# Rest of the index stage taken apart among the first projections, second heads moved among the next pair's tiles, TensorE's two long loops written out

## What is computed

```python
q, k, v, ga, qi, ki, wi, u, gb = _project(x, pos, w_in)      # one combined projection, 2048 -> 7248
I[t, s] = sum_h w[t, h] * relu(qi[t, h] . ki[s])              # 16 index heads of width 64
idx = top_k(causal(I), k)                                     # k = 128 (prompt), 256 (samples)
a = softmax(q . k[idx] / sqrt(128)) @ v[idx]                  # 8 heads of 128
p = pool_mix(u)                                               # trailing means, per-group map
y = LayerNorm(alpha * x + w_out @ [a * silu(ga); p * silu(gb)])
```

## Time and profile before

| | us |
|---|---|
| Runs (median, lowest, highest) | 1290.25, 1288.89, 1293.27 |
| Profiled execution | 1291.14 |
| Its span, first to last instruction | 1289.3 |
| Mean granted TensorE clock | 0.966 of full |

### The profile page before, as it was taken

One profiled execution on the slowest core, in us unless ns is written; L12 is line 12 of the kernel. 1 busy time (PEld: TensorE's weight loads), 2 busy tenths in 40 slices (PEclk: granted clock), 3 DMA queues, 4 the chain that ended last, 5 costly groups with the idle time before them and its releaser, 6 DMA issues.

```text
span 1289.3 us, 27399 instructions
## 1 busy us (share of the span) xinstructions
PE 1208.1 (94%) x10300; PEld 1109.7 (86%) x10300; DVE 592.3 (46%) x1080; ACT 358.9 (28%) x664; POOL 348.6 (27%) x150
## 2 busy tenths in 40 slices
PE   7899976989899999989998999999999999999995
PEld 6787755989899989989997888897888979999992
DVE  3555569986118404730763352342432643232326
ACT  4233332213222312232233232322232242212210
POOL 2322210333233323323331122112212223333320
PEclk8999987989999999989998999999999999999996
DMA  8522230322233223313334777667777757322203
GB/s 247 130 73 77 58 89 1 100 75 77 63 100 92 75 73 94 96 54 84 92 89 156 236 259 233 226 229 243 244 245 238 244 180 243 93 83 81 80 0 139
DMA packets 197976, 170.56 MB, mean 132 GB/s; under 512 B 19890, under 2 KB 178538, under 8 KB 196658
## 3 DMA queue, kind: packets, MB, share of 16 engines
q1 hardware_dynamic: 184458, 160.48, 40.2%
q10 hardware_dynamic: 13424, 8.67, 2.4%
HBM read 159.47 MB, written 9.74 MB: 131 GB/s over the span
## 4 chain that ended last, share of the span: by engine, by line
PE 75%; DVE 12%; issue 8%; ACT 2%; DMA 1%; DVEq 0%; ACTq 0%; SPq 0%
PE acc L1008 54%; PE bank L1222 5%; PE bank L1239 3%; PE acc L1312 2%; PE bank L1065 2%; DVE scoreP L1569 2%; DVE top L1565 2%; PE bank L1168 2%; PE bank L1149 1%; PE acc L1366 1%; DVE rot L1496 1%; DVE top L1604 1%; PE acc L1268 1%; DVE scoreS L1607 1%; DVE y L1915 1%
## 5 line engine op out<-in xcount | busy, mean ns | idle before, releaser
L597 POOL TENSOR_TENSOR wL<-rawW,wH 128x1024 fp32r<-128x1024 f32 (+1 forms) x146 | 348.4, 2387 | 892.4 <-ACT wH L619 892.4
L1008 PE MATMUL acc<-actH,wH 128*128 128x272 f32 (+1 forms) x2304 | 497.1, 297 | 10.2 <-issue 9.2
L1008 PE MATMUL acc<-actH,wL 128*128 128x272 f32 (+1 forms) x2304 | 481.4, 291 | 0.0
L1008 PE MATMUL acc<-actL,wH 128*128 128x272 f32 (+1 forms) x2304 | 480.2, 290 | 0.0
L1008 PEld LDWEIGHTS acc<-actH,wH 128*128 128x128 f32 (+1 forms) x2304 | 366.3, 191 | 31.5 <-issue 29.4
L1008 PEld LDWEIGHTS acc<-actL,wH 128*128 128x128 f32 (+1 forms) x2304 | 366.5, 191 | 0.0
L1008 PEld LDWEIGHTS acc<-actH,wL 128*128 128x128 f32 (+1 forms) x2304 | 364.1, 191 | 0.0
L619 ACT ACTIVATE wH<-rawW 128x1024 fp32r<-128x1024 f32 (+1 forms) x146 | 153.8, 1055 | 270.3 <-PE acc L1008 257.2
L1222 PE MATMUL bank<-sq,kPage 128*128 128x128 f32 x512 | 70.8, 282 | 9.0 <-issue 4.9
L1222 PEld LDWEIGHTS bank<-sq,kPage 128*128 128x128 f32 x512 | 56.8, 143 | 21.4 <-issue 16.3
L1627 DVE SCALAR_TENSOR_TENSOR gate<-tanhC,raw 128x544 f32<-128x544 f32 x8 | 5.8, 723 | 146.7 <-ACT raw L810 146.7
(11 more groups left out here) (206 smaller groups left out, 1029.1 us busy)
## 6 DMA issues: line engine op xcount, KB each, us to landing
rawW<-in_w_in SPq DMA_DIRECT2D x112, 512.0 KB, 3.8
kPage<-in_cache_k SPq DMA_DIRECT2D x64, 512.0 KB, 4.7
vPage<-in_cache_v SPq DMA_DIRECT2D x64, 512.0 KB, 4.8
rawW<-in_w_out SPq DMA_DIRECT2D x32, 512.0 KB, 4.0
y<-in_x_prompt SPq DMA_DIRECT2D x4, 1024.0 KB, 9.3
out_y_prompt<-y SPq DMA_DIRECT2D x8, 512.0 KB, 2.8
xnat<-in_x_prompt SPq DMA_DIRECT2D x2, 1024.0 KB, 7.6
xnat<-in_x_prompt ACTq DMA_DIRECT2D x2, 1024.0 KB, 11.2
```

What stands on the lines that cost most here:

```text
L597: pool.tensor_tensor(wL[:, slot, :, 0:width], rawW[:, slot, :, 0:width], wH[:, slot, :, 0:width].bitcast(F32), ALU.subtract).then_inc(stag ...
L1008: last = pe.matmul(acc[t.slot][0:width, e, 0:HT], w[:, u.slot, k, 0:width], a[:, kk, e * HT:(e + 1) * HT], start=(half == 0 and k == 0 and ...
```

## The change

The memory plan is reordered (two holes of 64 and 160 columns are put in) so that the buffers of the pair stage that are used early lie clear of the index stage's. The rest:

```diff
@@ banks: the index rest and the first pair's value transposes share one rotation; every pair has its own
+        zb = banks.stage([..., "R0", "T2", "R1", "T3", "v0", "vs0", "R2", "T4", "R3", "T5",
+                          "R4", "T6", "R5", "T7", "v1", "vs1", "R6", "R7", "Rn", "S0", "S1", "Sn"], four)
@@ SP: gate tiles follow the value tiles
+            for j in range(2):
+                load_tile(w_view, GA0 + j * P, TILE_C + 2 + j)
+            order = ((K0, 0), (Q0, 0), (K0, 1), (Q0, 1), (V0, 2), (V0, 3), (GA0, 2), (GA0, 3))
...
+            sp.wait_ge(exp_ready, 32)
+            key_pages(0, 1, None)
             sp.wait_ge(c_done, 1)
-            key_pages(0, 1, None)
+            key_pages(0, 2, "K3a")
             sp.dma_start(wtab[:], windows).then_inc(wtab_in, 16)
+            mask(0, None)
+            key_pages(0, 3, "K7a")
             unit(4)
@@ ACT: among the index rest
+                if n == 1:
+                    high(TILE_C + 3, 0)
+                    values(0, 0)
+                if n == 3:
+                    copy_tile(1, raw[:, 1])
+                    high(TILE_C + 3, 1)
+                if n == 5:
+                    high(TILE_C + 4, 0)
+                    values(1, 0)
+                if n == 7:
+                    gate_tile(2, 0)
+                    high(TILE_C + 4, 1)
@@ ACT: before the cached attention
-            for m in range(3):
+            copy_tile(0)
+            for m in range(8):
                 key_copied("a", m)
-            key_copied("a", 3)
+            exps(0)
             high(TILE_B + 2, 0)
...
@@ PE: the index rest
+            unit(TILE_C, 0)
...
+            index_products(zb, names[0:2], 1)
+            unit(TILE_C, 1, quarters=(0,))
+            index_products(zb, names[2:4], 1)
+            unit(TILE_C, 1, quarters=(1,))
+            index_products(zb, names[4:6], 1)
+            unit(TILE_C + 1, 0, quarters=(0,))
+            rows_scored(0)
+            unit(TILE_C + 1, 0, quarters=(1,))
+            rows_scored(1)
+            copied(TILE_C)
+            by_token("v", 0, 0, raw[:, 0])
...                       (rows_scored(2) to (7), one quarter between two; v1 after the fifth)
+            unit(TILE_C + 3, 0, quarters=(0,))
             b = zb("Rn") ...
+            unit(TILE_C + 3, 0, quarters=(1,))
             (S0, S1)
+            unit(TILE_C + 3, 1, quarters=(0,))
             (Sn)
+            unit(TILE_C + 3, 1, quarters=(1,))
@@ PE: a pair, written out four times; j = TILE_C + 4 + 8 * i; tiles K0 Q0 K1 Q1 V0' V1' gate0' gate1'
+                unit(j, 0); unit(j, 1); unit(j + 1, 0)
+                pe.wait_ge(head_ready, 4 * i + 2); by_token("k", 0, i, kT[:, 0])
+                unit(j + 1, 1); unit(j + 2, 0)
+                pe.wait_ge(head_ready, 4 * i + 3); scores(0)
+                unit(j + 2, 1); unit(j + 3, 0)
+                pe.wait_ge(head_ready, 4 * i + 4); by_token("k", 1, i, kT[:, 1]); turned(0, 0); turned(0, 1)
+                unit(j + 3, 1); values_of(0, 0); turned(0, 2); values_of(0, 1); turned(0, 3)
+                unit(j + 4, 0); values_of(0, 2); values_of(0, 3)
+                pe.wait_ge(head_ready, 4 * i + 5); scores(1)
+                if last: unit(TILE_B, 1); (all of turned(1, .), values_of(1, .)); return
+                unit(j + 4, 1); unit(j + 5, 0)
+                copied(j + 4); by_token("v", 0, i + 1, raw[:, 0]); turned(1, 0); turned(1, 1)
+                unit(j + 5, 1); values_of(1, 0); turned(1, 2); values_of(1, 1); turned(1, 3)
+                unit(j + 6, 0); values_of(1, 2); values_of(1, 3)
+                copied(j + 5); by_token("v", 1, i + 1, raw[:, 1])
+                unit(j + 6, 1); unit(j + 7, 0); unit(j + 7, 1)
@@ PE: "a" of the cached attention, and the loop over groups
-                if m in (0, 2, 4, 5):
-                    quarter((0, 0, 1, 1, 2, 3)[m])
...
-            with pe.Fori(0, LOOPS) as g:
-                group(g, False)
-            group(LOOPS, True)
+            for g in range(GROUPS):
+                group(g, g == LOOPS)
@@ DVE
-            EARLY = (0, 2, 4)
+            EARLY = (0, 2, 3, 5, 6)
...
+            copied(TILE_C + 2); make_gate(0)          (between R7 and Rn)
...
-            with dve.Fori(0, TOPK_P // ROUND - len(EARLY)) as i:
+            picks(2); copied(TILE_C + 3); make_gate(1); picks(3)
+            rotated(0, kT, 0, 0); picks(3)
+            rotated(1, qT, 0, 0); picks(TOPK_P // ROUND - len(EARLY) - 8)
...                                                   (keepP as before, then the pairs, written out)
+                late = i == 3
+                if i:
+                    rotated(0, kT, 0, i); pick_keys(3)
+                    rotated(1, qT, 0, i); pick_keys(2 if late else 3)
                 softmax(0)
+                rotated(2, kT, 1, i); gated(0, (0, 1)); rotated(3, qT, 1, i); gated(0, (2, 3))
                 softmax(1)
+                if not late:
+                    pick_keys(4)
                 gated(1, range(TT))
+                if not late:
+                    copied(TILE_C + 10 + 8 * i); make_gate(0)
+                    copied(TILE_C + 11 + 8 * i); make_gate(1); pick_keys(1)
```

More of the change, by code:

```diff
@@ new lines, in heads @@
+                keys_out(1)
+                copy_tile(j + 3, qT[:, 1])
+                probs_turned(0, (2, 3))
+                high(TILE_C + j + 5, 1)
+                if last:
+                    act.wait_ge(head_ready, 4 * i + 5)
+                    sample_part(qS, 1, qT)
+                    exps(1)
+                    probs_turned(1, range(TT))
+                    return
+                high(TILE_C + j + 6, 0)
+                act.wait_ge(head_ready, 4 * i + 5)
+                sample_part(qS, 1, qT)
@@ L820, in _ @@
+                high(TILE_C + j + 9, 0)
+                act.wait_ge(gate_ready, 2 * i + 3)
+                gate_tile(j + 7, 1)
+                high(TILE_C + j + 9, 1)
+            for i in range(4):
+                heads(i, i == 3)
             for t in range(TT):
@@ L1089, in pages_turned, with rows_scored, by_token @@
                 full(b, last)
+            def rows_scored(n):
+                b, b2 = zb(f"T{n}"), zb(f"R{n}")
+                dst = take(b2)
+                pe.wait_ge(bank_free[b.slot], b.read)
+                for a in range(PAGES // 2):
+                    last = pe.matmul(dst[:, a * P:(a + 1) * P], kiPT[:, n % 2, a, :],
+                                     qiS[:, :, :, n * NT:(n + 1) * NT].rearrange("p e h t -> p (e h) t"),
+                                     start=True, stop=True)
+                full(b2, last)
+                if n + 2 < NB:
+                    pages_turned(n + 2)
+            def by_token(name, X, i, src):
+                for part, lo, hi in (("", 0, NP_), ("s", NP_, T)):
+                    b = cb(f"{name}{part}{X}", i)
+                    dst = take(b)
+                    for n, at in enumerate(range(lo, hi, P)):
+                        last = pe.transpose(dst[0:min(P, hi - at), n * P:(n + 1) * P], src[:, at:min(at + P, hi)], ident)
+                    full(b, last)
+            unit(TILE_C, 0)
             pe.wait_ge(kip_in, 16 * NB * PAGES)
@@ new lines, in heads @@
+                turned(0, 0)
+                turned(0, 1)
+                unit(j + 3, 1)
+                values_of(0, 0)
+                turned(0, 2)
+                values_of(0, 1)
+                turned(0, 3)
+                unit(j + 4, 0)
+                values_of(0, 2)
+                values_of(0, 3)
+                pe.wait_ge(head_ready, 4 * i + 5)
+                scores(1)
+                if last:
+                    unit(TILE_B, 1)
+                    turned(1, 0)
+                    turned(1, 1)
+                    values_of(1, 0)
+                    turned(1, 2)
+                    values_of(1, 1)
+                    turned(1, 3)
+                    values_of(1, 2)
+                    values_of(1, 3)
+                    return
@@ L1199, in _ @@
+                unit(j + 4, 1)
+                unit(j + 5, 0)
+                copied(j + 4)
+                by_token("v", 0, i + 1, raw[:, 0])
                 turned(1, 0)
                 turned(1, 1)
+                unit(j + 5, 1)
                 values_of(1, 0)
@@ L1616, in _ @@
             own.step(dve.tensor_copy(keepP[:, 0:P], causal))
-            dve.wait_ge(consts_in, 32)
             own.step(dve.tensor_scalar(halfscale[:], halfscale[:], 0.5, None, ALU.mult))
-            rounds = TOPK_S // ROUND // 4
-            with dve.Fori(0, 4) as i:
-                own.enter(i, 2 * rounds + 4 * 3 + 8)
-                def make_gate(X):
-                    dve.scalar_tensor_tensor(gate[:, X, :], tanhC[:], 1.0, raw[:, X, :], ALU.add, ALU.mult
-                                             ).then_inc(gate_ready, 1)
+            own.wait()
+            for i in range(4):
                 def softmax(X):
```

346 lines of the change are left out of this document (180 added, 166 removed).

## The result

The changed kernel takes 1261.8 us (median of 4 runs, 1260.4 to 1263.2) beside 1289.6 us for the kernel before on the same chip: a ratio of 0.977 (0.975 to 0.979). The forecast was 1258.5 us. The profiled executions are 1291.1 and 1260.4 us, with spans of 1289.3 and 1258.6 us; the granted clock rose from 0.966 to 0.976.

A forecast was written before the change was run, and what follows sets the result against it. PE's own line of work was taken to bound the kernel; -18.4 - 19.6 + 6.8 + 5 - 6.5 = -32.7 us took the profiled 1291.14 to 1258.4 us, the median forecast being 1258.5 us, range 1248 to 1270 us.

The forecast's parts named there:

- A: Index rest to the first K1: reordered work removes PE's waits for DVE's sums, -18.4 us (bounds -31 and -12).
- B: Pair loop written out: three stops, the clock after them and waits for probabilities go, -19.6 us (-13 to -21).
- C: One round more before softmax 0 in pairs 1 and 2 makes PE wait for K1, +6.8 us (0 to +8).
- D: "a" without its quarters: thin steps and waits for key pages, +5 us (+1 to +11).
- E: Groups' loop on PE written out: two stops and 1.5 us of clock go, -6.5 us (-5 to -8).
- 59.8 us: DVE's chain from the last sample score, near 240 us, to K1 rotated in the first pair, so at 299.8 us.
- three rotations at 4.8: DVE's rotations before the first K1, POOL beside them at worst, plus gaps: 14.4 us of DVE's chain.
- some 2 us: PE's forecast stand before K0 and again before Q0 in the first pair, with 8 us before K1.
- PE waits 2.6 us in each of two pairs: Wait before K1 in pairs 1 and 2, from one 2.84 us round more before softmax 0.
- 0.8 us each for the clock: Added in pairs 1 and 2 for the lower clock, on top of the 2.6 us wait in each.
- Rival 2: DVE's chain is longer, weighings meeting POOL in the index rest, more low clock, "a" at its upper end: 1267 us, 22%.
- 17 us: Length of "a" from the end of its 4.09 us stop: eight steps 15.2 us, plus waits for pages.

The follow-up runs named there:

- early_three: Changed kernel with two prompt rounds fewer among DVE's index-stage sums (three instead of five), done after the sample scores instead: 1270.1 us, ratio 0.986.
- more_rounds: Changed kernel with two prompt rounds more ahead of the last sample scores: 1252.8 us, ratio 0.974.
- pair_pe_only: Kernel before with PE's loop over the first four pairs alone written out: 1282.6 us, ratio 0.994.
- both_pe: Kernel before with PE's pair loop and groups' loop both written out, nothing moved: 1268.4 us, ratio 0.984.
- c_two_rounds: Changed kernel with two sample rounds instead of three before softmax 0 in pairs 1 and 2, the third behind softmax 1: 1247.3 us, ratio 0.967.
- pool_away: Changed kernel with ACT's two high parts after K1's copy moved behind K1's keys and the first probabilities: 1245.5 us, ratio 0.965.
- sp_order: Changed kernel with SP's loads before the cached attention reordered, mask, key pages and history earlier: 1257.2 us, ratio 0.974.
- group_pe_only: Kernel before with PE's loop over the first three groups alone written out: 1284.0 us, ratio 0.994.
- pe_group_loop: Changed kernel with PE's loop over the groups put back as a loop, nothing else: 1275.3 us, ratio 0.988.

## Why the prediction was right, and where it was not

The total was right to 2 us out of 31 in the profiled executions and to 3.3 us in the medians, and that was luck in part: A and B gave 7.7 us more than forecast, C and D cost 10.1 us more. The stretches give each step, B as what is left of its stretch when C and the clock behind the first K1 are taken off. By steps, forecast and measured in the profiled executions:

| Step | forecast | measured |
|---|---|---|
| A index rest to the first K1 | -18.4 | -23.4 |
| B pair loop | -19.6 | -22.3 |
| C a round before softmax 0 | +6.8 | +12.3 |
| D "a" | +5 | +9.6 |
| E groups' loop | -6.5 | -6.9 |
| sum | -32.7 | -30.7 |

**A** was right in mechanism: PE's own path stands to 240 us, and DVE's chain from the last scores sets K1, which early_three and more_rounds show from both sides. The gain at K1 is 13.93 + 12.05 = 26.0 us, and the lower clock behind the wait takes 2.6 us back (9.57 us from K1's transposes to the next value products, 6.94 before), where I took 1.5. The term mis-sized is "59.8 us" for the chain: it took 55.7 us, from 237.99 to 293.68. It began 2 us earlier; of "three rotations at 4.8" (the four pieces named there add up to 5.1) two took 2.9 us, as their multiplies met no piece of POOL, and one met two and took 6.9 (K0's had luck: a piece ended at 256.75 us, as its first multiply began, at 256.71); and the mask, which I had taken at 2.57 us, ran in 0.76, with no piece of POOL beside it (before, one ran from 261.81 to 264.21 us):

```profile
281.88 0.76 DVE L1754 TENSOR_SCALAR keepP<-scoreP 128x1152 bf16<-128x1152 f32 x1
```

K0's and Q0's forecast waits of "some 2 us" did not come, as the chain began earlier and their rotations met nothing.

**B**: the stops and the clock, 15.3 us, are exact by pair_pe_only. The rest of the 22.3 us, 7.0, is the second heads' end; I took four waits of 1.07 us, 4.3. Two runs that have neither a stop nor a wait for K1 from the second pair on show it directly: from the second K1 to the third is 112.18 us in both_pe, with the old end, and 110.21 in c_two_rounds, 2.0 us less a pass, and the last stretch (K1 to the first key page) is 1.0 less. The wait is only a part of that; in both_pe it is

```profile
445.69 0.46 PE L1168 MATMUL bank<-probT,vN 128*128 128x128 f32 x2 [1.16 <-ACT probT L633]
```

and the other 0.8 us of a pass were not in my sum.

**C** is the step that failed in size: "PE waits 2.6 us in each of two pairs", and it was 4.33 and 4.31, and "0.8 us each for the clock", and it was 3.7 for both. The round came as forecast (2.84 us); what I left out is that it also moves K1's rotation in time, against POOL's pieces. It met two of them instead of one: 2.69 and 2.75 us for multiplies of 0.71. Either edit alone, c_two_rounds or pool_away, takes the wait away, to 0.31 us or less. Neither the round nor the meeting is therefore the whole cause; the wait needs both. Rival 2 had this mechanism, but at the weighings of the index rest; there it did not occur. All eight weighings took 680 to 694 ns, as no piece of POOL lay beside them (and rival 2's terms of 4, 3 and 3 us give 1268.5 us, not 1267):

```profile
L1695 DVE TENSOR_TENSOR relu<-relu,wiB x8: 680/683/694, 195.6 to 227.6; 128x512 f32<-128x512 f32 x8
```

That was luck: the last weighing ended at 228.30 us, and a piece began at 228.56; no run shows what a meeting would have cost there. The sum that the prediction had made by the Trainium skill's page "SBUF — State Buffer", section "Who interferes with whom", had the rule right and the place wrong. The section's sentence that the later instruction waits for the whole of the other agrees with the trace at K1: in the second pair POOL's piece ended at 406.80 us, and the multiply that had begun behind it, 0.71 us alone, ended at 407.37.

**D** had two faults. The eight steps took 18.1 us (672.52 to 690.62) for the "17 us" of the forecast, close; but from my own numbers the step should have been 17 + 12.05 - 26.6 = +2.5 us, since the moved tile costs no more than its 12.05 us elsewhere; measured +3.6. The other 6.1 us lie behind "a", from 690.62 to 703.80 us, 13.2 us where the kernel before took 7.1. Of these, 4.3 us are the two waits for loads that stand later in SP's order, 1.54 us for the page and 2.79 for the history; the rest is not taken apart, but the granted clock is 0.87 there. I had counted SP's queue for the key pages and not for what the first group needs. sp_order gave 4.6 of them back.

**E** was right within 0.5 us, by group_pe_only too. That is luck in part: the same loop cost 11 us in pe_group_loop, and I had no way to tell which price would hold.

Seen from the whole, both_pe is the plainest finding: two loops of one engine written out, with nothing moved, give 23.2 of the change's 27.8 us. The moving of work gained 23.4 us in A and 7 in B and lost most of it, 21.9 us, to C and D, two of whose causes were cheap to mend.

## What to carry to other kernels

When work is moved, follow what else shifts in time with it: the rotation that now meets POOL's pieces, and each load that stands behind in the same queue. The waits of 4.3 us at PE cost 1.5 to 2.1 us more in clock behind them, so four small edits of order together were worth as much as the change. Before rearranging anything, try writing out the long loops of the engine that bounds the kernel, all of those whose ends show such stops: the price of one that is left can change with the code around it. The short loop over the index tiles (L1068), left as it was, shows no such stop in the kernel before; all of PE's idle time from 50 to 175 us ends on DVE, 1.06 us at most.

## What the runs showed of the hardware

- The same jump back in the same loop body cost 2.30 and 2.58 us in one kernel and 3.69 and 4.13 us in another, where only other code of PE's had been changed, and 3.64 and 3.74 us in a third. The pair loop's three jumps went from 3.02, 3.08 and 3.06 us to 2.63, 2.57 and 2.56 us when only the groups' loop was written out. I had expected a constant. The fetch itself took longer at the long stops (an estimate of 2 us for each of two packets against 1.2 us for one); why, no run asks.
- Two of POOL's pieces back to back took a little longer as well: 5.12 us for two, beside 2.39 us for one, while DVE's multiplies beside them took 2.62 and 2.85 us.
- ACT's and DVE's loops turning over at the same places cost nothing that shows in the pair stage: in both_pe PE's only idle time in a pass of 112.18 us is the 1.16 us above.
- A stop is not always followed by the lower clock: behind the groups' first stop before (2.30 us) the granted clock was 0.83 for 10 us, behind the second (2.58 us) 1.00.
